# A hybrid encoder step on one core: the last stage joined to the experts' block, some of its rows gathered early, four of its tiles summed by TensorE

## The chip, the cores and the metric

The kernel is one program on one core of a Trainium2 chip. The metric is the device time of one execution in microseconds (us); lower is better. The kernel before was timed in 3 runs, and one more execution was recorded by the profiler.

## The reference

One inference step of a one-layer encoder for 1024 prompt rows and 64 sample rows, 1088 rows of 1024 values. Three branches (stick-breaking attention, gated linear attention, cross-attention into a memory) are gated, merged and projected, and give `h`. Then every row goes to two of 32 experts (the best of 4 groups, the best two of its 8 experts), and the result is normed once more:

```python
h = h + moe(rmsnorm(h))       # sum over the row's two experts e_k of
                              #   w_k * ((silu(x @ wg[e_k]) * (x @ wu[e_k])) @ wd[e_k])
y = rmsnorm(h) * norm_final   # outputs y_prompt (1024 rows), y_sample (64 rows)
```

The change concerns the last two lines alone: the sum of the two experts' rows and the final norm.

## The kernel before, in words

Rows are cut into nine tiles of 128 partitions (`NT = 9`; the last tile, number 8, has the 64 sample rows, `rows_of(t)`). The program is a chain of stages. A stage (`Stage`, line 51) has its own semaphores and one block of five instruction streams, one for each engine; at its end all engines meet at barriers and the semaphores are cleared (`Stage.clear`, line 63).

The last stage but one (lines 1754 to 2677) merges the branches, routes the rows and computes the experts. After routing, each expert has a slot of 128 rows in the DRAM tensor `expert_rows` (`ysd`); `sidx[k]` holds, for every row of the step, the line of `ysd` at which its k-th expert's result stands (`slots`, line 2629, run on VectorE within expert 14), and `wts` holds its two weights. Slots from 32 on are for experts with more than 128 rows; they are worked off by the loop in `further` (line 1778), whose bodies run only if there are such rows. In the profiled execution there were none.

For each expert n POOL gathers the slot's rows (`xe`, line 1892), SP loads the weights in halves (`raw`, 1 MB each, order `halves` on line 1715: gate, up of expert n, down of expert n-1; eight buffers, freed by the semaphore `used`, which TensorE raises when it has used a half), ScalarE rounds each half to `hig` (line 2238), VectorE subtracts to get `low` (line 2508), and TensorE multiplies in three passes (lines 2066 to 2068 and 2092 to 2094). ScalarE copies the expert's result out of PSUM into `ye` and stores it into `ysd` from its own DMA queue (line 2314). The last expert's result goes out in two halves (`last_out`, lines 2316 to 2326). At the end of the block ScalarE waits until all stores have landed (lines 2367 and 2368).

The last stage (lines 2687 to 2744) runs over the nine tiles:

- SP loads the final gain `gf` (line 2696), and stores each tile when it is scaled (line 2700).
- POOL gathers for each tile two sets of rows, `ya` and `yb`, from `ysd` by `sidx` (line 2708): 18 gathers of 128 rows of 4 KB (64 rows for tile 8).
- VectorE forms `ya * w0 + h` (line 2728) and then `yb * w1 + ya` (line 2731), both f32 over 1024 columns (`add`).
- ScalarE squares and sums the row, takes logarithm and exponential of the half for the inverse root (lines 2717 to 2721).
- VectorE multiplies the row with its root and `gf` into `yo` (line 2737, `scale`), one tile behind `add`.

## Time and profile before

| | us |
|---|---|
| median of 3 runs | 1832.4 |
| lowest, highest | 1829.63, 1832.93 |
| profiled execution, its own time | 1830.22 |
| span of the profiled execution, first to last instruction | 1828.5 |

| engine | busy, us | share of the span |
|---|---|---|
| TensorE (PE) | 1751.3 | 96% |
| VectorE (DVE) | 1055.0 | 58% |
| ScalarE (ACT) | 867.6 | 47% |
| GpSimd (POOL) | 111.7 | 6% |

The shares are means over stages with different limits; TensorE is idle in the last fortieth of the span or so. PEld is TensorE's weight load, PEq, ACTq, POOLq and SPq are the engines' sequencers, which issue DMAs. PEclk is the clock that TensorE was granted, as a share of full speed. The DMA share is the mean busy share of the core's 16 DMA engines; it can come out a little over 1. "Landing" is the time from the issue of a DMA until its semaphore says that all of it has arrived. Times within the trace count from the start of the span.

### The profile page before, as it was taken

How to read it: one execution, taken by the hardware profiler on the slowest of the kernel's cores; microseconds unless marked ns; L12 is line 12 of the kernel's file. 1: busy time of each engine (PE TensorE's matmuls, PEld its weight loads, DVE VectorE, ACT ScalarE, POOL GpSimd, SP SyncE). 2: the span in 40 equal slices, each digit the busy share in tenths (PEclk: the TensorE clock that was granted, in tenths of full speed). 3: DMA queues.
4: the chain of work that ended last, by engine and by line, in shares of the span. 5: the costliest groups of instructions: out<-in, count | busy, mean ns of one | idle time of the engine just before them, and what ended most of it. 6: DMA issues, size and time to landing. Idle time of an engine off the chain costs nothing. (4 is left out here: it accounts for less than half of the span.)

```text
span 1828.5 us, 25561 instructions
## 1 busy us (share of the span) xinstructions
PE 1751.3 (96%) x10338; PEld 1557.1 (85%) x10338; DVE 1055.0 (58%) x1285; ACT 867.6 (47%) x1122; POOL 111.7 (6%) x130
## 2 busy tenths in 40 slices
PE   8999999999999999999999999989999999999980
PEld 7888887989898899999999988878888888888870
DVE  5336664533354432142333155678988998898967
ACT  4225555332444331121122133258888888888753
POOL 0010000000000010000000000010001110000003
PEclk9999999999999999999999999989999999999995
DMA  5231111102022122222222152189999999999968
GB/s 190 82 107 41 30 31 42 30 24 74 24 73 81 47 73 80 65 87 70 75 80 65 35 186 82 53 316 400 416 412 410 414 416 419 417 415 408 415 228 304
DMA packets 139321, 329.85 MB, mean 180 GB/s; under 512 B 13674, under 2 KB 91334, under 8 KB 114501
## 3 DMA queue, kind: packets, MB, share of 16 engines
q1 hardware_dynamic: 123556, 272.69, 40.2%
q0 software_dynamic: 10896, 38.74, 5.6%
q10 hardware_dynamic: 4752, 16.78, 2.3%
q8 instruction: 84, 1.38, 0.3%
q14 instruction: 33, 0.27, 0.0%
HBM read 286.08 MB, written 39.87 MB: 178 GB/s over the span
## 5 line engine op out<-in xcount | busy, mean ns | idle before, releaser
L2508 DVE TENSOR_TENSOR low<-raw,hig 128x2048 fp32r<-128x2048 f32 x192 | 431.7, 2286 | 57.6 <-ACT hig L2238 57.4
L2238 ACT ACTIVATE hig<-raw 128x2048 fp32r<-128x2048 f32 x192 | 360.6, 1916 | 31.3 <-DMA raw<-in_w_e_gate_dram 14.9
L2066 PE MATMUL bank<-hig,xel 128*128 128x512 f32 x512 | 202.5, 396 | 0.5 <-DVE xel L2579 0.5
L2068 PE MATMUL bank<-hig,xeh 128*128 128x512 f32 x512 | 199.9, 390 | 0.0
L2067 PE MATMUL bank<-low,xeh 128*128 128x512 f32 x512 | 199.3, 389 | 0.0
L70 PE MATMUL bank<-xhi,glo 128*128 128x384 f32 (+1 forms) x552 | 180.6, 327 | 1.9 <-PEq L65 1.9
L72 PE MATMUL bank<-xhi,ghi 128*128 128x384 f32 (+1 forms) x552 | 180.8, 327 | 0.0
L71 PE MATMUL bank<-xlo,ghi 128*128 128x384 f32 (+1 forms) x552 | 180.5, 327 | 0.0
L70 PE MATMUL gproj<-xhi,glo 128*128 128x384 f32 (+1 forms) x384 | 130.1, 339 | 0.0
L72 PE MATMUL gproj<-xhi,ghi 128*128 128x384 f32 (+1 forms) x384 | 125.3, 326 | 0.0
L71 PE MATMUL gproj<-xlo,ghi 128*128 128x384 f32 (+1 forms) x384 | 125.2, 326 | 0.0
L2068 PEld LDWEIGHTS bank<-hig,xeh 128*128 128x128 f32 x512 | 96.1, 188 | 20.5
L2066 PEld LDWEIGHTS bank<-hig,xel 128*128 128x128 f32 x512 | 96.6, 189 | 19.6 <-DVE xel L2579 0.8
L2067 PEld LDWEIGHTS bank<-low,xeh 128*128 128x128 f32 x512 | 96.3, 188 | 19.0
L2401 DVE TENSOR_TENSOR tm<-sg,bank 128x384 f32<-128x384 f32 (+1 forms) x42 | 22.3, 531 | 152.5 <-PE bank L72 152.5
L70 PEld LDWEIGHTS bank<-xhi,glo 128*128 128x128 f32 x552 | 104.2, 189 | 2.0 <-issue 2.0
L71 PEld LDWEIGHTS bank<-xlo,ghi 128*128 128x128 f32 x552 | 104.2, 189 | 0.0
L72 PEld LDWEIGHTS bank<-xhi,ghi 128*128 128x128 f32 x552 | 104.0, 188 | 0.0
L2092 PE MATMUL bank<-hig,htl 128*128 128x512 f32 x256 | 102.4, 400 | 0.0
L2094 PE MATMUL bank<-hig,hth 128*128 128x512 f32 x256 | 100.0, 390 | 0.0
L2093 PE MATMUL bank<-low,hth 128*128 128x512 f32 x256 | 99.9, 390 | 0.0
L2172 ACT ACTIVATE sg<-bank 128x384 f32<-128x384 f32 (+1 forms) x63 | 29.7, 471 | 145.6 <-PE bank L72 136.6
(432 smaller groups left out, 3556.6 us busy)
## 6 DMA issues: line engine op xcount, KB each, us to landing
raw<-in_w_e_gate_dram SPq DMA_DIRECT2D x64, 1024.0 KB, 8.3
raw<-in_w_e_up_dram SPq DMA_DIRECT2D x64, 1024.0 KB, 8.5
raw<-in_w_e_down_dram SPq DMA_DIRECT2D x64, 1024.0 KB, 7.8
graw<-in_w_in_dram SPq DMA_DIRECT2D x39, 512.0 KB, 3.7
expert_rows<-ye ACTq DMA_DIRECT2D x31, 512.0 KB, 8.3
xt<-in_x_prompt_dram SPq DMA_DIRECT2D x16, 512.0 KB, 3.6
expert_rows<-nil POOLq DMA_DIRECT2D x16, 512.0 KB, 4.1
braw<-in_w_branch_dram SPq DMA_DIRECT2D x24, 256.0 KB, 3.0
```

The source lines that it names most:

```text
L70: nc.tensor.matmul(out, wl, xh, start=(opens and i == 0), stop=False)
L71: nc.tensor.matmul(out, wh, xl, start=False, stop=False)
L72: last = nc.tensor.matmul(out, wh, xh, start=False, stop=(closes and i == len(parts) - 1))
L2066: nc.tensor.matmul(bank[:, :], xel[n % 2][:, kk, :], wh[:, k, :], start=(kk == 0), stop=False)
L2067: nc.tensor.matmul(bank[:, :], xeh[n % 2][:, kk, :], wl[:, k, :], start=False, stop=False)
L2068: last = nc.tensor.matmul(bank[:, :], xeh[n % 2][:, kk, :], wh[:, k, :], start=False, stop=(kk == KC - 1))
L2092: nc.tensor.matmul(bank[:, :], htl[n % 2][:, kk, :], wh[:, k, cols], start=(kk == 0), stop=False)
L2093: nc.tensor.matmul(bank[:, :], hth[n % 2][:, kk, :], wl[:, k, cols], start=False, stop=False)
L2094: last = nc.tensor.matmul(bank[:, :], hth[n % 2][:, kk, :], wh[:, k, cols], start=False, stop=(kk == 3))
L2172: nc.scalar.activation(gate_of(i, g)[:, 0:m], src[:, 0:m], ACT.Sigmoid).then_inc(gated, 1)
L2238: nc.scalar.activation(hig[q % HI][:, :], raw[q % RAW][:, :], ACT.Copy).then_inc(high, 1)
L2508: nc.vector.tensor_tensor(low[q % RAW][:, :], raw[q % RAW][:, :], hig[q % HI][:, :].bitcast(F32), ALU.subtract).then_inc(lowed, 1)
```

## The change

The last stage's block is joined to the experts' block: no clearing and no barriers lie between them. Each engine's part stands behind its `further`, and the order is kept by semaphores. TensorE raises `closed` when its own work is done; SP then loads `gf`, ScalarE loads its table and VectorE begins. ScalarE raises `written` when every store into `ysd` has landed.

- **Gathers.** `LATE` is 3712, the first line of expert 29. For tiles 0 to 5 (`TWICE = 6`) POOL gathers twice. First, once the last two weight halves have landed and the stores of experts 0 to 28 too, it gathers by `sidx` with `bounds_check = LATE - 1`: lines beyond are left as they are. These rows go into buffers of the experts' block that have become free (`rows_at` gives each buffer and the value of `used` that frees it). After `written` it gathers again by `lidx`, in which the lines below `LATE` have 2^20 added and are so out of range. Tiles 6 to 8 are gathered once, after `written`. That makes 12 gathers before and 18 after `written`, where there were 18.
- **`slots`** computes `lidx`: two more small operations with a `drain` each, and two more copies, on VectorE.
- **Sums.** Tiles 1, 3, 5 and 7 (`ON_PE`) are summed by TensorE in PSUM: identity times `h`, plus a diagonal of the weights times `ya`, plus another times `yb`, each in two halves of 512 columns, all f32. VectorE builds the eight 128x128 diagonals `dg`. ScalarE and VectorE then read these tiles' sums from PSUM. VectorE adds the other five tiles as before, and scales two tiles behind instead of one.
- **PSUM** is declared as four tensors of 1024 columns in place of eight of 512; the addresses are the same.
- **Buffers** of `further`'s loop are moved to other places.

The diff, without the declarations that only move buffers:

```diff
-    psum = [top.enter_context(nc.psum_tensor(f"bank{i}", [P, 512], F32)) for i in range(8)]
-    PA, PB, TB, Z0, Z1, A0, A1, OB = psum
+    banks = [top.enter_context(nc.psum_tensor(f"banks{i}", [P, 1024], F32)) for i in range(4)]
+    PA, PB, TB, Z0, Z1, A0, A1, OB = [banks[i // 2][:, 512 * (i % 2):512 * (i % 2) + 512] for i in range(8)]
...
+    lidx = [at("lidx", [P, NT], I32, CON + 1024 + 64 * k) for k in range(2)]
...
+    LATE = (NE - 3) * P
+    TWICE = 6
+    spent = lambda kind, n, h: place[kind, n, h] + 1
+    rows_at = [(e0, 0), (e0 + 4096, 0), (e0 + 8192, spent("u", NE - 2, 1)), (e0 + 16384, spent("u", NE - 2, 1))]
+    for kind, h in (("g", 0), ("g", 1), ("u", 0), ("u", 1)):
+        q = place[kind, NE - 1, h]
+        rows_at += [(raw_at[q % RAW] + 4096 * i, q + 1) for i in range(2)]
+        if kind == "u":
+            rows_at += [(hig_at[q % HI] + 4096 * i, q + 1) for i in range(2)]
+    rows_at += [(e0 + 12288, spent("u", NE - 1, 1)), (e0 + 20480, spent("u", NE - 1, 1))]
+    assert len(rows_at) == 2 * NT
+    ya = [at("ya", [P, D], F32, rows_at[2 * t][0]) for t in range(NT)]
+    yb = [at("yb", [P, D], F32, rows_at[2 * t + 1][0]) for t in range(NT)]
+    ys_ = [nc.alloc_semaphore(name=f"rows_in{t}") for t in range(NT)]
+    yo = [at("yo", [P, D], F32, 4096 * i if i < FULL else OS) for i in range(NT)]
+    gf = at("gf", [P, D], F32, OS + 4096)
+    junk = at("junk", [P, D], F32, OS + 8192)
+    ON_PE = [1, 3, 5, 7]
+    dg = at("dg", [P, 2 * len(ON_PE), P], F32, OS + 12288)
+    landed = lambda t: 64 if t < TWICE else 32
     fours = lambda t: t[:, :].rearrange("p (k n) -> p k n", k=4)
...
+            sp.wait_ge(closed, 1)
+            sp.dma_start(gf[:, :], io["norm_final"].partition_broadcast(P)).then_inc(norm_in, 16)
+            for t in range(NT):
+                r = rows_of(t)
+                sp.wait_ge(finished, t + 1)
+                sp.dma_start(yp[t * P:t * P + r, :] if t < FULL else ysm[:, :], yo[t][0:r, :]).then_inc(returned, 16)
+            sp.wait_ge(returned, 16 * NT)
...
+            pool.wait_ge(found, 1)
+            pool.wait_ge(s0, 16 * (LATE // P + 1) // 2)
+            pool.wait_ge(s1, 16 * (LATE // P // 2))
+            for q in range(len(halves) - 2, len(halves)):
+                pool.wait_ge(loaded[q % RAW], 16 * (q // RAW + 1))
+            for t in range(TWICE):
+                r = rows_of(t)
+                for k, dst in enumerate((ya, yb)):
+                    pool.wait_ge(used, rows_at[2 * t + k][1])
+                    pool.indirect_dma_start(dst[t][0:r, :], None, ysd[0:LATE, :],
+                                            bass.IndirectOffsetOnAxis(ap=sidx[k][0:r, t:t + 1], axis=0),
+                                            bounds_check=LATE - 1, oob_is_err=False).then_inc(ys_[t], 16)
...
+            pool.wait_ge(written, 1)
+            for t in range(NT):
+                r = rows_of(t)
+                if t < TWICE:
+                    pool.wait_ge(ys_[t], 32)
+                for k, dst in enumerate((ya, yb)):
+                    rows = (lidx if t < TWICE else sidx)[k]
+                    pool.indirect_dma_start(dst[t][0:r, :], None, ysd,
+                                            bass.IndirectOffsetOnAxis(ap=rows[0:r, t:t + 1], axis=0),
+                                            bounds_check=SLOTS - 1, oob_is_err=False).then_inc(ys_[t], 16)
...
+            pe.sem_inc(closed, 1)
+            pe.wait_ge(written, 1)
+            pe.wait_ge(diagonal, 1)
+            for j, t in enumerate(ON_PE):
+                for half in range(2):
+                    out, c = banks[j][:, 512 * half:512 * half + 512], slice(512 * half, 512 * half + 512)
+                    if half == 0:
+                        pe.wait_ge(ys_[t], landed(t))
+                    nc.tensor.matmul(wide(out), ident[:, :], hrow(t, P)[:, 4 * half:4 * half + 4, :], start=True, stop=False)
+                    nc.tensor.matmul(out, dg[:, 2 * j, :], ya[t][:, c], start=False, stop=False)
+                    last = nc.tensor.matmul(out, dg[:, 2 * j + 1, :], yb[t][:, c], start=False, stop=True)
+                last.then_inc(added, 1)
...
+            act.sem_inc(written, 1)
+            act.wait_ge(closed, 1)
+            nc.scalar.preload_act_table_set("natural_log_exp_and_others")
+            for t in range(NT):
+                R = slice(0, rows_of(t))
+                if t in ON_PE:
+                    act.wait_ge(added, ON_PE.index(t) + 1)
+                    total = banks[ON_PE.index(t)]
+                else:
+                    act.wait_ge(summed, t + 1 - sum(u < t for u in ON_PE))
+                    total = ya[t]
+                nc.scalar.activation(junk[R, :], total[R, :], ACT.Square, scale=D ** -0.5, accum_out=stat[R, t:t + 1])
+                act.drain()
+                nc.scalar.activation(stat[R, 16 + t:17 + t], stat[R, t:t + 1], ACT.Ln, bias=eps[R, :])
+                act.drain()
+                nc.scalar.activation(stat[R, 32 + t:33 + t], stat[R, 16 + t:17 + t], ACT.Exp, scale=-0.5).then_inc(inverted, 1)
...
+                nc.vector.tensor_scalar(isov[:, :, :], eid[:, :, :], float(LATE), float(1 << 20), ALU.is_lt, ALU.mult)
+                ve.drain()
+                nc.vector.tensor_tensor(isov[:, :, :], isov[:, :, :], eid[:, :, :], ALU.add)
+                ve.drain()
                 for k in range(2):
-                    last = nc.vector.tensor_copy(sidx[k][:, :], eid[:, :, k])
+                    nc.vector.tensor_copy(sidx[k][:, :], eid[:, :, k])
+                    last = nc.vector.tensor_copy(lidx[k][:, :], isov[:, :, k])
                 last.then_inc(found, 1)
...
-    ya = [at("ya", [P, D], F32, OS + 8192 * i) for i in range(NT)]
-    yb = [at("yb", [P, D], F32, OS + 8192 * i + 4096) for i in range(NT)]
-    yo = [at("yo", [P, D], F32, 4096 * i) for i in range(NT)]
...
-    with Stage(nc) as ctx:
...
-            for t in range(NT):
-                r = rows_of(t)
-                for k, dst in enumerate((ya, yb)):
-                    pool.indirect_dma_start(dst[t][0:r, :], None, ysd,
-                                            bass.IndirectOffsetOnAxis(ap=sidx[k][0:r, t:t + 1], axis=0)).then_inc(ys_[t], 16)
...
+            ve.wait_ge(closed, 1)
             def add(t):
                 r = rows_of(t)
-                ve.wait_ge(ys_[t], 32)
+                ve.wait_ge(ys_[t], landed(t))
...
             def scale(t):
                 r = rows_of(t)
-                ve.wait_ge(rooted, t + 1)
-                nc.vector.scalar_tensor_tensor(out=yo[t][0:r, :], in0=ya[t][0:r, :], scalar=stat[0:r, 32 + t:33 + t],
+                ve.wait_ge(inverted, t + 1)
+                total = banks[ON_PE.index(t)] if t in ON_PE else ya[t]
+                nc.vector.scalar_tensor_tensor(out=yo[t][0:r, :], in0=total[0:r, :], scalar=stat[0:r, 32 + t:33 + t],
                                                in1=gf[0:r, :], op0=ALU.mult, op1=ALU.mult).then_inc(finished, 1)
-            ve.wait_ge(g_in, 16)
-            for t in range(NT + 1):
-                if t < NT:
+            for j, t in enumerate(ON_PE):
+                for k in range(2):
+                    last = nc.vector.tensor_scalar(dg[:, 2 * j + k, :], ident[:, :], wts[:, t, k:k + 1], None, ALU.mult)
+            last.then_inc(diagonal, 1)
+            ve.wait_ge(norm_in, 16)
+            for t in range(NT + 2):
+                if t < NT and t not in ON_PE:
                     add(t)
-                if t >= 1:
-                    scale(t - 1)
+                if t >= 2:
+                    scale(t - 2)
```

## Rows read from the trace of the kernel before

**Rows 1.** Busy by windows: us; PE, PEld, DVE, ACT, POOL busy; PEclk, DMA share, GB/s

```profile
1469.00:1481.00 12.00, 12.00 (x56) 9.99 (x55) 11.70 (x16) 9.24 (x9) 0.00 (x0) 1.00 1.01 417
...
1764.50:1773.80 9.30, 9.30 (x44) 7.53 (x43) 5.23 (x4) 3.20 (x4) 0.00 (x0) 1.00 0.00 1
...
1780.00:1781.00 1.00, 0.00 (x0) 0.00 (x0) 0.00 (x0) 0.00 (x0) 0.00 (x0) 0.54 0.24 88
...
1790.00:1796.00 6.00, 0.00 (x0) 0.00 (x0) 5.82 (x5) 2.48 (x5) 4.73 (x5) 0.50 1.00 367
...
1800.00:1812.00 12.00, 0.00 (x0) 0.00 (x0) 11.78 (x11) 5.50 (x15) 4.67 (x5) 0.50 1.03 420
```

**Rows 2.** The chain that ended last, in order of time: start us, us, what

```profile
1783.01 0.94 POOL ya L2708
...
1784.26 5.45 DMA yb<-expert_rows,sidx
...
1821.40 1.06 ACT junk L2717
...
1823.22 1.28 DVE yo L2737
```

**Rows 3.** Second addition, line 2731: duration ns min/median/max, starts, forms

```profile
L2731 DVE SCALAR_TENSOR_TENSOR ya<-yb,wts,ya x9: 1275/1283/1285, 1791.2 to 1820.1; 128x1024 f32<-128x1024 f32 x8, 64x1024 f32<-64x1024 f32 x1
```

**Rows 4.** Gathers of the last stage, line 2708: duration ns min/median/max, starts, landing

```profile
L2708 POOL DMA_INDIRECT ya<-expert_rows,sidx x9: 919/948/1397, 1783.0 to 1803.8; - x9
...
L2708 POOL DMA_INDIRECT yb<-expert_rows,sidx x9: 910/949/1066, 1784.3 to 1805.0; - x9
...
  issue: 5.2, 17
...
DMA to landing us min/median/max: 4.5/5.8/12.4
```

**Rows 5.** Timeline, end of experts: start us, us, engine line op [idle before <-releaser]

```profile
1763.57 0.39 PE L2066 MATMUL bank<-hig,xel 128*128 128x512 f32 x1
...
1763.96 4.48 DVE L2508 TENSOR_TENSOR low<-raw,hig 128x2048 fp32r<-128x2048 f32 x2
...
1764.09 1.92 ACT L2238 ACTIVATE hig<-raw 128x2048 fp32r<-128x2048 f32 x1 [0.61 <-DMA raw<-in_w_e_down_dram]
...
1773.81 0.34 ACTq L2314 DMA_DIRECT2D expert_rows<-ye  x1
...
1777.65 0.39 PE L2094 MATMUL bank<-hig,hth 128*128 128x512 f32 x1
...
1778.70 0.34 ACTq L2326 DMA_DIRECT2D expert_rows<-ye  x1
```

**Rows 6.** Gathers of the experts' loop, line 1892: duration ns min/median/max

```profile
L1892 POOL DMA_INDIRECT xe<-ffn_rows,toks x32: 942/1368/3187, 1202.1 to 1714.4; - x32
```

**Rows 7.** Landing: the experts' stores (line 2314), the last (line 2326), gf (line 2696)

```profile
DMA to landing us min/median/max: 2.6/8.3/10.6
...
DMA to landing us min/median/max: 2.0/2.0/2.0
...
DMA to landing us min/median/max: 3.8/3.8/3.8
```

**Rows 8.** f32 matmuls of 512 columns: timeline of four records; durations of line 1129

```profile
561.48 1.88 PE L1129 MATMUL gout<-pT,mn 128*128 128x512 f32 x4
...
L1129 PE MATMUL gout<-pT,mn x16: 592/592/595, 561.5 to 644.6; 128*128 128x512 f32 x16
```

**Rows 9.** Busy time by windows at the kernel's start; columns as in rows 1

```profile
12.00:13.00 1.00, 1.00 (x4) 0.77 (x3) 1.00 (x2) 1.00 (x1) 0.00 (x0) 0.50 1.02 393
...
15.00:16.00 1.00, 1.00 (x5) 0.82 (x4) 0.73 (x2) 0.87 (x2) 0.00 (x0) 0.80 1.06 389
```

**Rows 10.** ScalarE reading 1024 columns of PSUM, line 1293 (form 128x1024)

```profile
L1293 ACT ACTIVATE osq<-gout,stat x6: 360/1114/1116, 394.8 to 522.7; 128x1024 f32<-128x1024 f32 x4, 128x128 f32<-128x128 f32 x2
```

**Rows 11.** A small operation of slots, line 2641

```profile
L2641 DVE TENSOR_TENSOR eid<-eid,isov x1: 178/178/178, 1475.5 to 1475.5; 128x18 f32<-128x18 f32 x1
```

More of the change, by code:

```diff
@@ L1769, in build @@
                 ctx, "o", "t in g u d turned copied hidden silued mult hturned hcopied down read out passed")
+        norm_in, diagonal, summed, added, inverted, finished, returned, closed, written = sems(
+            ctx, "z", "norm_in diagonal summed added inverted finished returned closed written")
+        ctx.held += ys_
+        yp = io["out0"].rearrange("b t d -> (b t) d")
+        ysm = io["out1"].rearrange("b t d -> (b t) d")
         g_in, b_in, x_in, kept = [g_in0, g_in1], [b_in0, b_in1], [x0, x1], [kept0, kept1]
@@ L2677, in _ @@
             further(ve, body)
-    ya = [at("ya", [P, D], F32, OS + 8192 * i) for i in range(NT)]
-    yb = [at("yb", [P, D], F32, OS + 8192 * i + 4096) for i in range(NT)]
-    yo = [at("yo", [P, D], F32, 4096 * i) for i in range(NT)]
-    gf = at("gf", [P, D], F32, 36864)
-    junk = at("junk", [P, D], F32, 40960)
-    with Stage(nc) as ctx:
-        g_in, summed, rooted, finished, stored, *ys_ = sems(
-            ctx, "z", "g_in summed rooted finished stored " + " ".join(f"y{t}" for t in range(NT)))
-        block = ctx.enter_context(nc.Block())
-        yp = io["out0"].rearrange("b t d -> (b t) d")
-        ysm = io["out1"].rearrange("b t d -> (b t) d")
-        @block.sync
-        def _(sp):
-            sp.dma_start(gf[:, :], io["norm_final"].partition_broadcast(P)).then_inc(g_in, 16)
-            for t in range(NT):
-                r = rows_of(t)
-                sp.wait_ge(finished, t + 1)
-                sp.dma_start(yp[t * P:t * P + r, :] if t < FULL else ysm[:, :], yo[t][0:r, :]).then_inc(stored, 16)
-            sp.wait_ge(stored, 16 * NT)
-        @block.gpsimd
-        def _(pool):
-            for t in range(NT):
-                r = rows_of(t)
-                for k, dst in enumerate((ya, yb)):
-                    pool.indirect_dma_start(dst[t][0:r, :], None, ysd,
-                                            bass.IndirectOffsetOnAxis(ap=sidx[k][0:r, t:t + 1], axis=0)).then_inc(ys_[t], 16)
-        @block.scalar
-        def _(act):
-            nc.scalar.preload_act_table_set("natural_log_exp_and_others")
-            for t in range(NT):
-                R = slice(0, rows_of(t))
-                act.wait_ge(summed, t + 1)
-                nc.scalar.activation(junk[R, :], ya[t][R, :], ACT.Square, scale=D ** -0.5, accum_out=stat[R, t:t + 1])
-                act.drain()
-                nc.scalar.activation(stat[R, 16 + t:17 + t], stat[R, t:t + 1], ACT.Ln, bias=eps[R, :])
-                act.drain()
-                nc.scalar.activation(stat[R, 32 + t:33 + t], stat[R, 16 + t:17 + t], ACT.Exp, scale=-0.5).then_inc(rooted, 1)
-        @block.vector
-        def _(ve):
```

12 lines of the change are left out of this document (6 added, 6 removed).

## The prediction, made before the changed kernel ran

> **What bounds the kernel now.** I read the windows over the end first, then the chain, then the timeline around the hand-over, and last the groups of single lines. The experts' block is bound by TensorE until 1778.0 and the change leaves that part alone, but for some small operations in `slots`. From the last weights on the DMA engines have nothing to do: share 0.00 from 1764.5 to 1773.8, while TensorE works through the last expert [rows 1]. Then come the hand-over and the last stage. The reader should see in the chain that POOL's first gather starts at 1783.01, that its pair lands at about 1789.7 and that VectorE's last scaling starts at 1823.22 [rows 2]: with its 1.28 us it ends at 1824.5, and the span ends 4.0 us later, at 1828.5. So the last stage is 41.5 us from first gather to last VectorE instruction. In it VectorE is busy for 11.78 of 12 us [rows 1]: each tile costs it two additions and a scaling of 1.28 us each, nine tiles at 3.75 us [rows 2, 3]. POOL needs 0.95 us plus an idle 0.30 us for a gather, 2.5 us for a tile [rows 4], so it runs ahead.
>
> **The sum, part by part.** g is the start of POOL's first gather after the hand-over; times are those of the trace.
>
> Early gathers. Twelve, tiles 0 to 5. The last raw half has landed when ScalarE starts on it at 1764.09 [rows 5]; the stores of experts 0 to 28 landed well before, as that of 29 was issued two experts' time ago, and the buffers of tiles 4 and 5 come free when TensorE ends the first half of expert 31's `up`, at about 1763.6 [rows 5]. At 1.25 us each [rows 4] POOL issues them until 1779.3; at 1.37 + 0.30 us, the median of the gathers in the experts' loop [rows 6], until 1784.1. VectorE, whose work goes with the long ones, has two splits left until 1768.4 [rows 5], so I take 1780. They move up to 6.3 MB in DMA time that stood empty.
>
> The hand-over. Before: last store issued 1778.70, landed 2.0 us later [rows 5, 7], then the clearing of semaphores, the barriers, POOL's start at 1783.01. After: the store, two semaphores, POOL. With free DMA engines g would be 1781.2. But the stores of experts 30 and 31 (issued 1773.8 and, its last half, 1778.7 [rows 5]) now share the engines with gathers that fill them: 1.00 of the DMA share with gathers alone [rows 1]. Bounds for one store: 2.0 us alone, and 8.3 us, the median of those beside the weight loads [rows 7]. At 367 GB/s [rows 1] 5.7 MB of rows and 1.0 MB of stores take 18.3 us from 1764.5, until 1782.8. I take 3.3 us, g = 1782.5: 0.5 us won of 1.8. The Trainium skill, DMA: Bandwidth & Descriptors, section Queues, rings and completion order, has a DMA engine go round its queues a packet at a time. By that a store waits for about one packet of the gathers on each engine, near the short bound; the 8.3 us of this trace speak against it, so both stay.
>
> Late gathers. Eighteen in place of eighteen, twelve of them with nine rows in ten out of range. POOL's time for such a row isn't in the trace. The 64-row gathers took 0.91 to 0.92 us, as good as the 128-row ones [rows 4], so fewer rows hardly save; I take 1.25 us, bounds 0.9 and 1.67 [rows 6]. Landing from issue: 4.5 us at least for full ones [rows 4], 2.0 us for a small store; I take 3.5. Tile t's second gather starts at g + 1.25(2t+1): tile 0 is there at 1787.3, tile 1 at 1789.8, tile 3 at 1794.8, tile 5 at 1799.8. Tiles 6 to 8 are full and meet the output stores; before, landings reached 12.4 us [rows 4]. I take 7: tile 7 at 1808.3, tile 8 at 1810.8.
>
> TensorE's sums. Six f32 matmuls of 512 columns a tile. Such a matmul shows as two records; four records took 1.88 us and one takes 0.592, so (1.88 - 0.59) / 3 = 0.43 us from one to the next [rows 8]. A tile is 12 x 0.43 = 5.2 us at 2.4 GHz. But the granted clock fell to 0.5 at about 1780.1, 2 us after the last matmul [rows 1, 5], and at the start of the kernel it stood at 0.50 from 12 to 15 while matmuls ran without a pause, and was back in the slice from 15 to 16, by its 0.80 at about 15.4 [rows 9]. So I charge tile 1 with 4 us at half speed: 2 us more, 7.2 us, ready at 1797.0. Then tile 3 at 1802.2, tile 5 at 1807.4, tile 7 (waits for its rows, 1808.3) at 1813.5. TensorE, idle here before, is now as much a limit as POOL.
>
> ScalarE. From the square to VectorE's scaling 1.82 us [rows 2]; a 1024-wide read of PSUM took 1.11 us where the one of SBUF takes 1.06 [rows 2, 10], nothing to count. It takes the tiles in order, so tile 8 waits behind 7: 1815.3, 1817.1. `gf` and its table load now come before the rows (issue after `closed`, about 1779.5, landing 3.8 us later [rows 7]; VectorE waits for `gf` before its first addition, and has till 1787.3). If it lands 3 us late among gathers, nothing is lost.
>
> VectorE. Ten additions in place of eighteen and nine scalings: 19 x 1.25 = 24 us instead of 34. Its cover is gone: it now waits for TensorE's tiles through ScalarE. `add(8)` ends at 1813.5, `scale(6)` at 1814.8, `scale(7)` at 1816.6, `scale(8)` 1817.1 + 1.28 = 1818.4. The eight diagonals (128x128) fall into its empty time before 1787. The four small operations and two drains in `slots` cost some 0.9 us at 0.18 us each [rows 11], in a stretch where VectorE is 11.70 of 12 us busy and TensorE still never stops [rows 1]: hidden, at worst 0.9 us.
>
> The end. 4.0 us as now, plus 0.3 for stores that follow closer. 1818.4 + 4.3 = 1822.7 against 1828.5: **5.8 us less**. The profiled execution took 1830.2 us, so 1824.4; it is 2.2 us below the median of the runs shown, 1832.4. Against the median: **1826.6 us**, -0.32%. A measurement tells about 0.2% from nothing, 3.7 us. With the cheap ends of the bounds (store 2.0, landing 2.0 and 4.5) the end is some 10 us earlier: 1822.
>
> **Rivals.**
> A, slower: TensorE's clock stays at 1.2 GHz through its four tiles. It works in bursts with waits for rows between, after a long idle, and a drop needed only the 2 us of 1778 to 1780 [rows 1, 5]. Then a tile costs 10.3 us, tile 7 is ready at 1789.8 + 41.2 = 1831.0, `scale(8)` ends at 1836, the span at 1840: 12 us more, 1844. It decides from about 7.4 us a tile on: then the last scaling stands where it stood. For it: clock 0.50 over the whole last stage. Against it: dense matmuls brought the clock back in 4 us [rows 9], and by my sum TensorE hardly pauses. The Trainium skill, TensorE: Matmul & The Clock Gate, section Part 1: The HAM clock gate, says that sustained work brings the full clock back; the trace agrees at 15.4. 0.10.
> B, range-checked gathers are dear: 1.67 us each on POOL. Early ones until 1784.1, g = 1784.4, late ones 5 us more; tile 7's rows at 1815.2, its sum 1820.4, last scaling 1825.3, end 1829.6: 1833.5, no change, and slower beyond that price. For it: the median 1.37 us in the experts' loop, up to 3.19 [rows 6]. Against: 0.95 us in the last stage although VectorE was busy throughout [rows 1, 4]. The Trainium skill, GPSIMD Engine Reference, section Key points, says that GpSimd's ports to SBUF are shared with VectorE's two-input instructions. VectorE's additions have two inputs and the gathers beside them were short, so the trace bears it out only in part. 0.16, a third of it slower.
> C, the early gathers hold up the last stores: 8.3 us as in the weight stream [rows 7]. Last store down at 1787.0, g = 1787.2, end 4.7 us later than forecast: 1831.3, no change. For it: a DMA share of 1.00. Against: the backlog should be gone by 1783. 0.14.
> D, the twelve late gathers still move all their rows: then DMA is full, but 8.9 MB of gathers and 4.5 MB of stores at 420 GB/s [rows 1] are 32 us from g, 1814.5, still inside POOL's and TensorE's pace. 1 to 2 us less gain. 0.04.
>
> **How the numbers follow.** The forecast (with D) has 0.60, most of it between 1822 and 1828.7; B 0.16, C 0.14, A 0.10. Faster: 0.60 x 0.92 and a few hundredths of B and C make 0.60. Same: 0.24. Slower: A 0.10, a third of B 0.05 and 0.01 of C make 0.16. The range runs from 1821.5 to 1835.0: it holds the forecast with both ends of its bounds, C, and B at its price, and leaves out A, B at more than its price, and a gain over 11 us.
>
> **What the profile of after would show.** Twelve gathers from 1764 to 1780; DMA share near 1 there; the last store landing by 1782; the first late gather at 1782.5; late gathers 1.25 us apart; f32 records 0.43 us apart after some 4 us at 0.85; a chain that changes between TensorE, ScalarE and VectorE, with no 3.75 us period; last scaling ending near 1818. The prediction falls if records stay 0.85 us apart (A), if POOL's period is over 1.6 us (B), or if the first late gather starts after 1786 (C).

## The result and the profile after

The changed kernel is slower: over 20 timed executions of each kernel on the same chips the median went from 1830.97 to 1838.48 us, and the ratio is 1.0035 with a 95% interval of 1.0026 to 1.0043. The forecast was 0.32% faster, with a range up to 1835.0; both the sign and the range missed. The ratios here are taken over executions in the ordinary, fast state: a few single ones that took far longer (3479.3 us of the kernel before, 1918.84 of e2, 2517.09 and 4504.99 of e8) are left out of them, though not out of the medians. The profiled execution took 1836.51 us, its span 1834.9 (before: 1830.22 and 1828.5).

The first view is the busy time by windows of the changed kernel (columns as in rows 1).

```profile
1766.00:1768.00 2.00, 2.00 (x10) 1.65 (x9) 2.00 (x2) 0.53 (x1) 1.79 (x1) 1.00 0.00 0
1768.00:1770.00 2.00, 2.00 (x11) 1.43 (x10) 1.69 (x2) 0.00 (x0) 1.87 (x1) 1.00 0.71 178
1770.00:1780.00 10.00, 8.68 (x40) 6.90 (x39) 0.69 (x1) 2.88 (x5) 7.59 (x8) 1.00 0.88 290
1780.00:1790.00 10.00, 0.00 (x0) 0.00 (x0) 1.66 (x8) 1.28 (x1) 3.27 (x4) 0.55 1.01 397
1790.00:1800.00 10.00, 3.91 (x5) 1.83 (x6) 4.02 (x4) 1.65 (x4) 7.56 (x9) 0.50 0.18 43
1800.00:1810.00 10.00, 10.00 (x22) 4.22 (x21) 6.26 (x6) 3.80 (x9) 7.87 (x8) 0.92 0.54 149
1810.00:1820.00 10.00, 6.01 (x13) 2.47 (x12) 7.26 (x6) 5.75 (x16) 2.60 (x3) 0.93 0.97 369
```

Read the DMA share down the column. The empty stretch before the hand-over is filled as intended, though only from 1768 on. But a new hole has opened where there was none: 0.18 from 1790 to 1800 and 0.54 after it, where the kernel before had 1.00 and 1.03 [rows 1]. VectorE is no longer the busy engine there (4.02 and 6.26 of 10 us; it was 11.78 of 12 before [rows 1]). POOL is: 7.56 and 7.87 us, which with 0.30 us between gathers is all of its time.

The timeline around the hand-over (start us, us, engine, line):

```profile
1765.58 2.22 POOL L1937 DMA_INDIRECT ya<-expert_rows,sidx  x1 [49.20 <-DMA expert_rows<-ye]
1768.10 1.87 POOL L1937 DMA_INDIRECT yb<-expert_rows,sidx  x1 [0.30 <-issue]
...
1779.35 0.34 ACTq L2393 DMA_DIRECT2D expert_rows<-ye  x1
1779.41 1.00 POOL L1937 DMA_INDIRECT yb<-expert_rows,sidx  x1 [0.30 <-issue]
...
1782.03 1.06 POOL L1937 DMA_INDIRECT yb<-expert_rows,sidx  x1 [0.30 <-issue]
1788.47 1.28 ACT L2438 ACT_TABLE_LOAD   x1 [9.16 <-DMA expert_rows<-ye]
1789.21 1.00 POOL L1957 DMA_INDIRECT ya<-expert_rows,lidx  x1 [6.12 <-ACTq L2436]
```

Twelve early gathers (line 1937), nine of them issued before the last store at 1779.35. ScalarE then waits 9.2 us for that store and only then gives `written`; the first late gather (line 1957), called g as in the prediction, starts at 1789.21, 9.9 us after the store's issue, against 4.3 before (1783.01 less 1778.70, [rows 2, 5]).

The chain that ended last answers to rows 2:

```profile
1779.35 9.04 DMA expert_rows<-ye
...
1807.55 1.78 POOL ya L1957
1809.64 8.77 DMA yb<-expert_rows,sidx
1818.45 1.99 PE banks L2209 x2
...
1825.60 1.02 ACT junk L2447
...
1829.06 1.27 DVE yo L2780
```

Before, this chain was VectorE's additions and scalings. Now it is the store's landing, then POOL's gathers one behind the other, then the landing of tile 7's rows, then TensorE's sum of that tile. The group of the late gathers (answers to rows 4; its landings are those of full ones) and the landing of `gf` (the last line, from its own group; [rows 7]):

```profile
L1957 POOL DMA_INDIRECT ya<-expert_rows,lidx x6: 1001/1001/1018, 1789.2 to 1802.3; - x6
L1957 POOL DMA_INDIRECT yb<-expert_rows,lidx x6: 997/1000/1053, 1790.5 to 1803.6; - x6
L1957 POOL DMA_INDIRECT ya<-expert_rows,sidx x3: 963/999/1783, 1804.9 to 1811.0; - x3
L1957 POOL DMA_INDIRECT yb<-expert_rows,sidx x3: 948/1001/1053, 1806.2 to 1812.3; - x3
...
DMA to landing us min/median/max: 8.2/8.5/8.9
...
DMA to landing us min/median/max: 7.9/7.9/7.9
```

A gather that leaves out most of its rows costs POOL the same 1.00 us as a full one; what it saves is DMA time only. Its rows are there soon: TensorE began tile 1 at 1796.09, 3.0 us after that tile's second gather was issued at 1793.13. That is how the hole from 1790 to 1800 comes about: twelve nearly empty gathers (`lidx`) keep POOL for 12 x 1.31 = 15.7 us and give the DMA engines almost nothing, and the six full ones stand behind them. The DMA queues from 1764 to the end show that no row is moved twice (queue, kind: packets, MB, share); first the changed kernel, then the one before from 1780 on:

```profile
q0 software_dynamic: 4192, 8.92, 38.4%
```

```profile
q0 software_dynamic: 2464, 8.91, 48.6%
```

TensorE's sums, timeline of line 2209 to 2211; each row of two records is one f32 matmul of 512 columns:

```profile
1796.09 2.04 PE L2209 MATMUL banks<-mixT,ident 128*128 128x512 f32 x2 [17.40 <-DMA yb<-expert_rows,lidx]
1797.92 1.91 PE L2210 MATMUL banks<-ya,dg 128*128 128x512 f32 x2
...
1801.34 1.11 PE L2209 MATMUL banks<-mixT,ident 128*128 128x512 f32 x2
1802.28 1.02 PE L2210 MATMUL banks<-ya,dg 128*128 128x512 f32 x2
...
1818.45 1.99 PE L2209 MATMUL banks<-mixT,ident 128*128 128x512 f32 x2 [3.99 <-DMA yb<-expert_rows,sidx]
...
1821.95 1.04 PE L2211 MATMUL banks<-yb,dg 128*128 128x512 f32 x2
```

At half clock a matmul takes 1.71 us, at the full one 0.86. The clock rose after 5.2 us of work (granted clock 0.62 in the window 1800 to 1802, 1.00 from 1802 on). It fell again at the end of TensorE's wait of 3.99 us for tile 7's rows: 1.00 until 1818.5, 0.57 from 1818.5 to 1819, 0.50 until 1821.5.

### The profile page after: what moved, and what is told of

Its sections match the earlier page's. It is cut to its first block, busy times and chain, and to the rows that moved or that the text cites. A ratio compares the mean times of both kernels' runs of the same rounds, so it can differ in the third digit from the quotient of the medians.

```text
span 1834.9 us, 25681 instructions
## 1 busy us (share of the span) xinstructions
PE 1778.3 (97%) x10386; PEld 1569.0 (86%) x10386; DVE 1047.5 (57%) x1289; ACT 867.5 (47%) x1122; POOL 134.5 (7%) x142
## 4 chain that ended last, share of the span: by engine, by line
PE 59%; DMA 2%; issue 1%; POOL 1%; DVE 0%; ACT 0%; DVEq 0%; ACTq 0%; POOLq 0%
PE banks L70 7%; PE banks L72 7%; PE banks L71 7%; PE banks L2121 6%; PE banks L2123 6%; PE banks L2122 6%; PE banks L2149 3%; PE banks L2147 3%; PE banks L2148 3%; PE banks L2004 2%; PE banks L2006 2%; PE banks L2005 2%; PE banks L2107 2%; PE banks L2131 1%; PE banks L2034 1%
## 5 line engine op out<-in xcount | busy, mean ns | idle before, releaser
L2121 PE MATMUL banks<-hig,xel 128*128 128x512 f32 x512 | 202.5, 396 | 0.5 <-DVE xel L2662 0.5
L2123 PE MATMUL banks<-hig,xeh 128*128 128x512 f32 x512 | 199.9, 390 | 0.0
L2122 PE MATMUL banks<-low,xeh 128*128 128x512 f32 x512 | 199.3, 389 | 0.0
L70 PE MATMUL banks<-xhi,glo 128*128 128x384 f32 (+1 forms) x552 | 179.9, 326 | 1.9 <-PEq L65 1.9
L72 PE MATMUL banks<-xhi,ghi 128*128 128x384 f32 (+1 forms) x552 | 180.0, 326 | 0.0
L71 PE MATMUL banks<-xlo,ghi 128*128 128x384 f32 (+1 forms) x552 | 179.9, 326 | 0.0
L70 PEld LDWEIGHTS banks<-xhi,glo 128*128 128x128 f32 x552 | 103.6, 188 | 2.0 <-issue 2.0
L72 PEld LDWEIGHTS banks<-xhi,ghi 128*128 128x128 f32 x552 | 103.6, 188 | 0.0
L71 PEld LDWEIGHTS banks<-xlo,ghi 128*128 128x128 f32 x552 | 103.6, 188 | 0.0
L2147 PE MATMUL banks<-hig,htl 128*128 128x512 f32 x256 | 102.4, 400 | 0.0
```

What stands on the lines that cost most here:

```text
L70: nc.tensor.matmul(out, wl, xh, start=(opens and i == 0), stop=False)
L71: nc.tensor.matmul(out, wh, xl, start=False, stop=False)
L72: last = nc.tensor.matmul(out, wh, xh, start=False, stop=(closes and i == len(parts) - 1))
L2121: nc.tensor.matmul(bank[:, :], xel[n % 2][:, kk, :], wh[:, k, :], start=(kk == 0), stop=False)
L2122: nc.tensor.matmul(bank[:, :], xeh[n % 2][:, kk, :], wl[:, k, :], start=False, stop=False)
L2123: last = nc.tensor.matmul(bank[:, :], xeh[n % 2][:, kk, :], wh[:, k, :], start=False, stop=(kk == KC - 1))
```

## The experiments

The experts' block does the same work in all of them, early gathers aside, but ends at another time in each trace (the last store's issue, called s here, lies between 1777.1 and 1782.9), so profiled executions are compared from s to the end of the span. Each such figure comes from one execution. The verdict is the ratio to the kernel before on the same chip; it is not the quotient of the medians shown. Two theories stood against each other. S: the early gathers hold up the last store, and with it `written` and all the late gathers. O: the order of the late gathers, empty ones first and full ones last, wastes the DMA engines and brings tile 7's rows late.

| kernel | gathers issued before s | store landed after | g - s | end - g | end - s | median us | ratio to before (95%) |
|---|---|---|---|---|---|---|---|
| before | 0 | 2.0 | 4.3 | 45.5 | 49.80 | 1830.97 | 1 |
| after | 9 | 9.0 | 9.9 | 45.7 | 55.55 | 1838.48 | 1.0035 (1.0026 to 1.0043) |
| e1_no_early | 0 | 2.0 | 2.9 | 47.8 | 50.69 | 1831.62 | 0.9998 (0.9989 to 1.0007) |
| e2_early3 | 6 | 4.0 | 4.8 | 44.6 | 49.47 | 1831.88 | 0.9998 (0.9989 to 1.0007) |
| e3_join_only | 0 | 2.0 | 2.9 | 46.2 | 49.04 | 1830.21 | 0.9997 (0.9988 to 1.0005) |
| e4_no_pe | 10 | 8.8 | 9.7 | 45.5 | 55.15 | 1836.37 | 1.0027 (1.0017 to 1.0036) |
| e5_warm | 10 | 9.9 | 10.7 | 48.0 | 58.69 | 1837.86 | 1.0029 (1.0017 to 1.0041) |
| e6_mixed | 6 | 4.0 | 4.8 | 43.9 | 48.72 | 1829.02 | 0.9983 (0.9974 to 0.9992) |
| e7_split | 6 | 4.1 | 8.7 | 46.6 | 55.23 | 1836.69 | 1.0024 (1.0015 to 1.0034) |
| e8_mixed2 | 4 | 2.0 | 2.8 | 45.3 | 48.14 | 1830.75 | 0.9990 (0.9980 to 0.9999) |
| e9_half_stores | 0 | 2.0 | 2.9 | 43.0 | 45.89 | 1828.37 | 0.9980 (0.9970 to 0.9991) |
| e10_split4 | 6 | 3.7 | 4.5 | 43.2 | 47.69 | 1828.26 | 0.9983 (0.9974 to 0.9992) |
| e11_early4 | 8 | 7.9 | 8.8 | 46.7 | 55.51 | 1836.22 | 1.0025 (1.0015 to 1.0036) |
| e12_full_first | 9 | 8.8 | 9.6 | 39.4 | 49.06 | 1830.56 | 0.9992 (0.9983 to 1.0001) |

(In `before`, g is the first gather of the last stage.) Where the tiles go in their natural order and all outputs are stored, the end comes 44.6 to 48.0 us after g, whatever was gathered early and whoever sums: 45.5 before, 45.7 after. So the 5.75 us that the changed kernel loses from s on are almost all its late g (9.9 for 4.3), and nothing that the early gathers and TensorE were to bring behind g arrived.

**The three parts one by one.** The change joins the stages, gathers early, and sums on TensorE. e1 takes the early gathers away, e2 halves them, e3 leaves only the joining, e4 only takes TensorE's sums away (e3 and e4 also drop the semaphore `diagonal`).

```diff
-    TWICE = 6
-    ON_PE = [1, 3, 5, 7]
+    TWICE = 0            # e1; 3 in e2; 0 in e3; 6 in e4
+    ON_PE = [1, 3, 5, 7] # e1, e2; [] in e3 and e4
```

> The changed kernel with TWICE = 0: no gather before the last stores, all nine tiles gathered once after them; all else as changed. Theory S (the early gathers and the gain's load keep the DMA engines full until 1789, and the last store's landing goes from 2.0 to 9.0 us): the last store lands in about 2 us again, the first late gather starts near 1782.2 instead of 1789.2, tile 7's sum by TensorE is ready near 1817, span about 1826, that is some 8 us under the changed kernel and 2 us under the one before. Rival K (the sums on TensorE, with its clock at half speed twice, are what costs): the span stays above 1832 though the gathers start earlier.

> The changed kernel with TWICE = 3: six early gathers instead of twelve. Theory S: they are issued from 1765.6 to about 1775 and drained by about 1777, before the last two stores are issued, so these land in 2 to 3 us and the first late gather starts near 1782.5; tiles 0 to 2 are then there at once, tile 7 as in the run without early gathers; span 1825 to 1826. Rival K: above 1832. If the delay of the store does not depend on the backlog (any gather on that queue delays it), the first late gather starts near 1789 as with twelve.

> TWICE = 0 and no tile on TensorE: only the blocks are joined, VectorE adds all nine tiles. Theory S: first gather near 1782.2 against 1783.0 before, then the same 3.75 us a tile: span about 1827.5, 1 us under the kernel before. It gives the price of the barrier between the stages. Rival: joining costs by itself (queues or semaphores): span above 1830.

> The changed kernel with TWICE = 6 kept and no tile on TensorE. Theory S: first late gather near 1789.2 as changed, tile 0 at 1793.3, then nine tiles at 3.75 us and 1.8 us of ScalarE with the last scaling: last scaling ends near 1830, span about 1834, within 1 us of the changed kernel. Rival K: taking TensorE out brings the span to 1829 or less.

The chains of e1 and of e2, from the last store to the rows of tile 7:

```profile
1779.31 2.02 DMA expert_rows<-ye
...
1802.75 10.75 DMA yb<-expert_rows,sidx
```

```profile
1779.13 4.01 DMA expert_rows<-ye
...
1803.65 10.19 DMA yb<-expert_rows,sidx
```

Both ended later than S had them (1830.0 and 1828.6, where about 1826 was expected), and below rival K's 1832. All of the loss belongs to the early gathers: without them the changed kernel runs as the one before, with all twelve it loses 0.35%, and with TensorE's sums or without them (after and e4) the intervals overlap. Joining the stages brings the first late gather 1.4 us nearer to the store (2.9 for 4.3), but in e3 the span ends 4.55 us after the last scaling where it was 4.00, and e3 as a whole cannot be told from before. And e1 shows why TensorE brings nothing: VectorE has 5.61 us of work in 10 (1790 to 1800), yet the rows of tile 7 land 10.75 us after their gather, because the DMA engines are full. Its windows:

```profile
1790.00:1800.00 10.00, 7.44 (x12) 3.33 (x13) 5.61 (x5) 1.65 (x4) 7.90 (x7) 0.63 1.00 387
1800.00:1810.00 10.00, 9.89 (x24) 4.14 (x23) 6.86 (x6) 6.30 (x16) 5.43 (x5) 1.00 0.99 371
```

**Is DMA the bound of the last stage?** e9 is e1 with only 512 of the 1024 columns of the two row outputs stored; it leaves half of those outputs out.

```diff
-                sp.dma_start(yp[...] if t < FULL else ysm[:, :], yo[t][0:r, :]).then_inc(returned, 16)
+                sp.dma_start((yp[...] if t < FULL else ysm[:, :])[:, 0:512], yo[t][0:r, 0:512]).then_inc(returned, 16)
```

> As e1_no_early, but only the first 512 of the 1024 columns of each output row are stored (2.2 MB instead of 4.5 MB; the other half of the two outputs is left out); all gathers and sums stay. If the DMA engines are the limit of the last stage (share 0.99 to 1.00 from 1790 to 1810 in e1_no_early, tile 7's rows landing 10.7 us after their issue): tile 7's rows land some 5 us earlier, TensorE does not wait for them, and from the last store's issue to the end of the span it is 46 us instead of 50.7. If TensorE's or POOL's pace is the limit: 50 us or more.

From s to the end it took 45.89 us, 4.8 less than e1, and the median fell by 3.3 us. No engine but the DMA had less to do. The 2.23 MB less at the 387 GB/s of e1's window would be 5.8 us. So with VectorE relieved the DMA engines bound this stage. In the kernel before they ran at 1.00 and 1.03 in the same stretch [rows 1], behind a VectorE that never paused; that they stood close behind it there is argued from these shares, since the kernel before was not run with half of its stores.

**More work for TensorE's clock.** e5 is the changed kernel with nine more matmuls (`warm`), whose results are overwritten later: five behind `written`, four ahead of tile 7.

```diff
             pe.wait_ge(diagonal, 1)
...
+            warm(5)
             for j, t in enumerate(ON_PE):
+                if j == 3:
+                    warm(4)
```

> The changed kernel with nine f32 matmuls of 512 columns added on TensorE into the bank of tile 7, which is overwritten later: five after `written`, four before tile 7. In the changed kernel the granted clock was 0.50 when tile 1's rows came, and fell again in the 4.0 us wait for tile 7's rows, whose sum then took 7.1 us instead of 5.2. Theory (the second fall is worth 1.9 us, the first nothing, because tile 7 waits for its rows anyway): from the issue of the last store to the end of the span 53.7 us instead of 55.6, tile 1 in about 5.2 us instead of 7.5. Rival (the clock costs 4 us in all): 51.5 us. If the added matmuls do not hold the clock: 55.6 or more.

The first sum did run at the full clock, but 53.7 us from s to the end were expected and 58.69 came. Timeline of TensorE in e5:

```profile
1795.38 1.13 PE L2215 MATMUL banks<-mixT,ident 128*128 128x512 f32 x2 [0.29 <-DMA yb<-expert_rows,lidx]
...
1819.52 2.08 PE L2215 MATMUL banks<-mixT,ident 128*128 128x512 f32 x2 [4.43 <-DMA yb<-expert_rows,sidx]
```

Tile 7's rows landed 10.5 us after their issue at 1808.94, and the clock fell in the wait for them (0.64 in 1817 to 1818) in spite of the four matmuls ahead, which had ended at 1815.1. The two medians (1837.86 and 1838.48) differ by less than their spread. The clock in the first sum is off the path: what decides is when tile 7's rows are there, and whether the clock has fallen by then. That the sums before it, ended earlier, put their output stores in the way of these rows fits, but is argued only.

**What does the store wait for?** e7 keeps twelve early gathers but holds the six of tiles 3 to 5 back until the last store is issued; e11 has eight in the old place.

```diff
                     pool.wait_ge(used, rows_at[2 * t + k][1])
+                    if t == 3:
+                        pool.wait_ge(emptied, NE)    # e7, e10
```

> The changed kernel, where POOL's last six early gathers (tiles 3 to 5) wait until the last expert's result has left PSUM, so that they are issued just behind the last store instead of ahead of it. If the DMA engines serve what was queued first (a store waits for the bytes queued before it): the last store lands in about 4.0 us, as with six early gathers, though six more follow. If a store shares the engines with gathers whenever they were queued: 7 to 9 us. In the first case the first late gather is held up by POOL's own six gathers, starting 8 to 8.5 us after the store's issue instead of 9.9: span about 1 to 2 us under the changed kernel.

> The changed kernel with TWICE = 4: eight early gathers, all ahead of the last store. The landing of the last store has been 2.0 us with none and with four, 4.0 with six, 9.0 with twelve. If it waits for what is queued before it, two more gathers of 0.95 MB in all at 0.38 MB per us add 2.5 us: 6.0 to 6.7 us, first late gather 7 us after the store's issue. If there is a threshold instead of a backlog: 4.0 or 9.0.

The landing of the last store in e7 and in e11:

```profile
DMA to landing us min/median/max: 4.1/4.1/4.1
```

```profile
DMA to landing us min/median/max: 7.9/7.9/7.9
```

Six gathers behind the store do not touch it in e7 (4.1, as e2 with none behind: 4.0). Those issued before it do, and steeply: 2.0 with none or four, 3.7 to 4.1 with six, 7.9 with eight, 8.8 to 9.9 with nine or ten. That is S's mechanism. For e11, 6.0 to 6.7 us were expected from a backlog, and 4.0 or 9.0 from a threshold; 7.9 is neither. The bytes that the queues moved show why it is steep:

| kernel | gathers ahead of s | rows moved until s, MB | moved from s to the landing: rows, all, MB | landing, us |
|---|---|---|---|---|
| e8 | 4 | 1.89 | 0, 0.35 | 2.0 |
| e2 | 6 | 2.49 | 0.38, 1.36 | 4.0 |
| e7 | 6 | 2.56 | 0.45, 1.14 | 4.1 |
| e11 | 8 | 2.54 | 1.30, 2.44 | 7.9 |
| after | 9 | 2.54 | 2.49, 3.60 | 9.0 |
| e5 | 10 | 3.09 | 2.57, 3.70 | 9.9 |

An early gather moves 0.48 MB (3.84 MB for the eight of e11). Until s the engines got through about 2.5 MB of rows, that is five gathers, in e11 and the changed kernel alike; what is issued beyond that ahead of the store stands whole in front of it. In the changed kernel 1.8 MB of the nine gathers were left at s, and 2.49 MB of rows moved before the store landed, so there rows issued behind it went along with it. In e7, where 0.3 MB were left, hardly any did.

A short landing alone does not help. The landing of e7 was 4.9 us shorter than that of the changed kernel, but g came only 1.2 us sooner and the end 0.3 us. The timeline of POOL in e7 shows why:

```profile
1779.09 1.00 POOL L1939 DMA_INDIRECT ya<-expert_rows,sidx  x1 [4.99 <-ACT ye L2393]
...
1785.62 1.00 POOL L1939 DMA_INDIRECT yb<-expert_rows,sidx  x1 [0.30 <-issue]
1786.93 1.00 POOL L1959 DMA_INDIRECT ya<-expert_rows,lidx  x1 [0.30 <-issue]
```

The six moved gathers occupy POOL until 1786.6, and the late ones, empty first, follow at the same 1.31 us: tile 7's second gather was issued 29.3 us after s, in the changed kernel 30.3. What counts is when POOL can begin its late gathers, and what stands in its queue ahead of the full ones. Where g itself moves, the end follows: e2 has g 4.0 us nearer to s than e11, and its end 6.0 us nearer.

**The order.** e12 is the changed kernel with the late gathers in another order, full tiles between empty ones (TensorE takes tiles 0, 1, 2 and 4 in it). SP, POOL, ScalarE and VectorE all follow the list.

```diff
-    ON_PE = [1, 3, 5, 7]
+    QUEUE = [6, 0, 7, 1, 8, 2, 3, 4, 5]
+    ON_PE = [0, 1, 2, 4]
...
-            for t in range(NT):
+            for t in QUEUE:
```

> The changed kernel with its twelve early gathers, so with the late last store (about 9 us, first late gather about 9.9 us after its issue), but the order of work after it is 6, 0, 7, 1, 8, 2, 3, 4, 5: the three tiles that move all their rows come first, when the DMA engines are empty and no output is being stored; TensorE's tiles stay at places 2, 4, 6 and 8 of the nine. Theory O (the changed kernel loses the second half of its time because its full gathers come last, behind output stores, and land 8.8 us after their issue): no wait for rows at the end, from the last store's issue to the end of the span about 49 to 50 us instead of 55.6, which puts it level with the kernel before (49.8). Theory S alone (the late store is the whole loss, the order does not matter): 55 us or more.

The chain of e12 (the store, then the first and the last of TensorE's matmuls) and its windows:

```profile
1781.94 8.81 DMA expert_rows<-ye
...
1798.64 2.05 PE banks L2210 x2
...
1815.83 1.46 PE banks L2212 x2
```

```profile
1790.00:1800.00 10.00, 1.35 (x2) 0.84 (x3) 1.73 (x2) 1.28 (x1) 6.58 (x7) 0.50 0.78 268
1800.00:1810.00 10.00, 10.00 (x20) 4.20 (x19) 6.39 (x6) 4.80 (x12) 7.59 (x8) 0.83 0.64 192
1810.00:1820.00 10.00, 10.00 (x25) 4.41 (x24) 9.01 (x8) 5.71 (x14) 4.63 (x4) 1.00 0.57 195
```

The store lands as late as in the changed kernel (8.8 us), all twelve early gathers are there, and still 6.5 us are gone: 49.06 us from s to the end instead of 55.55, a ratio of 0.9992 instead of 1.0035. From g to the end it is 39.4 us instead of 45.7, and the share in the first window after the hand-over went from 0.18 to 0.78. So both theories hold, each for its part. S is why the changed kernel is slower than the one before; O is why twelve early gathers and TensorE's sums gained nothing behind g; and mending either alone brings the kernel level with before (e2, e12). The next limit in e12 is TensorE, whose four sums follow each other without a pause from 1798.64 to 1817.3. That only the order of the full gathers matters, and not the choice of TensorE's tiles that had to go with it, was not taken apart.

**Versions that use this.** e6: three tiles early, full ones between the empty ones (order 0, 3, 1, 4, 2, 5, 6, 7, 8; TensorE 3, 4, 5, 7). e8: two early (order 0, 2, 1, 3, 4, 5, 6, 7, 8; TensorE 0, 1, 4, 6; two warming matmuls). e10: four early, the fourth held back as in e7 (order 0, 4, 1, 5, 2, 6, 3, 7, 8; TensorE 0 to 3).

> As e2_early3 (six early gathers), but the order of work is 0, 3, 1, 4, 2, 5, 6, 7, 8 in place of 0 to 8, with the tiles of TensorE at the same places in that order. Theory O (in e2_early3 POOL spent 7.8 us of DMA engines nearly empty, share 0.19 from 1784 to 1790, on gathers that move little, and then the full ones met the output stores at a share of 1.0, landing 9.0 us): the full gathers start earlier, landings fall to about 6 us, from the last store's issue to the end of the span 45 to 46.5 us instead of 49.5. Rival (POOL's 1.30 us a gather or TensorE's 5.2 us a tile is the limit, whatever the order): 49 us or more.

> A version meant to beat both: TWICE = 2 (four early gathers), order of work 0, 2, 1, 3, 4, 5, 6, 7, 8, TensorE sums tiles 0, 1, 4 and 6 (places 0, 2, 4 and 6, so that the last full tile is VectorE's), two added f32 matmuls to raise its clock. Theories S and O together: last store lands in 2 to 2.5 us, first late gather 3 us after its issue, landings 5 to 7 us, from the last store's issue to the end of the span 42 to 45 us, against 49.8 before and 55.6 changed. Rival: if the DMA engines are full anyway from 1790 on (8.9 MB of gathers less 1.9 MB, and 4.5 MB of stores), 47 us or more.

> A version meant to beat both: four early tiles, of which the fourth (two gathers) is issued just behind the last store; order of work 0, 4, 1, 5, 2, 6, 3, 7, 8; TensorE sums tiles 0 to 3, whose rows are mostly there. If a store waits for the bytes queued before it: it lands in 4.0 us as with three early tiles, the first late gather starts 4.8 us after its issue, and one more tile (0.95 MB, 2.4 us of DMA) is out of the late stretch: 46 to 47.5 us from the last store's issue to the end of the span, against 48.7 in e6_mixed, 49.8 before and 55.6 changed; ratio to the kernel before about 0.997. Rival: the two gathers behind the store hold it up too: first late gather 6 us or more after it, 48.5 us or more.

All three fell short of what was expected from s to the end: 48.72 us in e6 (45 to 46.5), 48.14 in e8 (42 to 45) and 47.69 in e10 (46 to 47.5, at a ratio of 0.997). With six early gathers the order is worth little: e6 differs from e2 in it alone (TensorE's tiles stand at the same places) and ends 0.75 us nearer to s; by the ratios (0.9983 and 0.9998) it may be up to 3 us, but their intervals overlap.

In e10's chain the last store and the landing of tile 7's rows, then its windows:

```profile
1777.11 3.69 DMA expert_rows<-ye
...
1801.68 8.62 DMA yb<-expert_rows,sidx
```

```profile
1780.00:1790.00 10.00, 3.21 (x4) 1.50 (x5) 0.33 (x2) 1.28 (x1) 6.79 (x8) 0.50 0.83 264
1790.00:1800.00 10.00, 10.00 (x22) 4.32 (x21) 5.83 (x5) 3.15 (x8) 7.87 (x8) 0.89 0.72 204
1800.00:1810.00 10.00, 10.00 (x24) 4.20 (x23) 7.94 (x7) 6.30 (x16) 4.39 (x5) 1.00 0.96 332
```

e10 and e6 beat both kernels by a little: 0.9983 (0.9974 to 0.9992), some 3 us below before and 10 us below the changed kernel. That is just under the 0.2% that was named as telling, though the interval leaves 1 out. e8 is at 0.9990 (0.9980 to 0.9999). Beside e11, which has the same four tiles early, e10 gains 8 us by the order and the held-back pair together. Even here POOL is busy without a pause and the DMA share is 0.72 from 1790 to 1800, so part of the DMA time that the early gathers won still goes unused while POOL works through its queue.

## Why the prediction was wrong, step by step

It had the last VectorE instruction end at 1818.4 and the span at 1822.7; they were 1830.3 and 1834.9. (Its base, a median of 1832.4 from three runs, was 1.4 us above the median over 20.) The 12.2 us between divide over its terms:

| term | predicted | measured | us |
|---|---|---|---|
| g, the first late gather | 1782.5 | 1789.21 | +6.7 |
| tile 7's rows, from g | 25.8 | 29.2 | +3.4 |
| TensorE's sum of tile 7 | 5.2 | 7.1 | +1.9 |
| end of that sum to the end of the last scaling | 4.9 | 4.8 | -0.1 |
| tail | 4.3 | 4.6 | +0.3 |

- **The hand-over (+6.7), the step that failed most.** I took 3.3 us for the store between bounds of 2.0 and 8.3; it took 9.0, beyond the upper end. Of the 6.7 us that is 5.7; 0.65 is a last store issued later in this trace, and 0.3 the way from landing to g (0.8 for 0.5). The bound was a median; the same row had landings of up to 10.6 [rows 7]. That is rival C's mechanism, to which I gave 0.14, at a g 2.0 us later than its 1787.2 (which, with the sum's own 0.5 us, should have been 1787.5). The reason that I set against it, a backlog gone by 1783, was wrong in its start: I let the rows move from 1764.5, but POOL's first gather started at 1765.58 and with the second took 2.22 and 1.87 us, beside VectorE's splits, and nothing moved before 1768; the share was 0.88, not 1.00, from 1770 to 1780. By s the engines had moved 2.54 MB of rows and 1.8 MB of those issued were left. As an estimate, the same 18.3 us counted from 1768 end at 1786.3, and `gf` (0.5 MB, left out of the sum) adds 1.4: 1787.7, near the 1788.39 at which the store landed. The Trainium skill, DMA: Bandwidth & Descriptors, section Queues, rings and completion order, lets the engines go round their queues by packets, which as I read it would put the store near 2 us; no run with six or more gathers ahead of it bears that out (3.7 to 9.9). The same section has the increment of a semaphore land only after the earlier writes of that DMA engine, whatever their queue. That the gathers ahead of the store count (e2, e11) and six behind it don't (e7) agrees with it; in the changed kernel rows issued behind the store went along with it too, so it is not the whole account.
- **From g to the end (40.2 us forecast, 45.7 measured).** I had the path right: tile 7's sum waits for its rows, and these for POOL's queue of eighteen gathers, which the early ones relieve of bytes but not of one instruction. What I did not ask is what the DMA engines do while twelve nearly empty gathers stand ahead of the six full ones. Their share was 0.18 for 10 us, and the full ones then met the output stores. With the full ones put between the empty ones (e12) it took 39.4 us. The other rows of the table are how these 5.5 us show in the sum.
- **Tile 7's rows (+3.4).** Their gather was issued 20.4 us after g instead of 18.75: fifteen steps of 1.31 us, not 1.25, and one gather of 1.78. They then took 8.8 us to land, not 7, beside the output stores, at a share of 0.97 from 1810 on. In e1, e2 and e11 the same landing took 10.2 to 10.75 us; with half of the stores (e9) it took 8.4 instead of e1's 10.75.
- **The clock (+1.9).** Tile 1 went as forecast, 7.9 us for 7.2, but was not on the path. The sum at the end was, and there I had charged nothing for the clock, since "TensorE hardly pauses": it had waited 3.99 us for the rows when the clock fell. Rival A, a clock that stays low, is out: tiles 3 and 5 took 5.15 us each.
- **Right:** the price of a sum at full clock (5.15 us for 5.2), the half clock on tile 1 (5.2 us of it, for 4), the diagonals hidden (done by 1782.6), small landings for tiles 0 to 5 (3.0 us for tile 1, where I took 3.5), `gf` 7.9 us on its way and not waited for. Rival B's price was small: 1.00 + 0.30 us a range-checked gather where the plain one of before took 0.95 + 0.30. Rival D is out: 8.92 MB through the gathers' queue, as before.
- **What was overlooked in the profile of before.** Rows 1 show the last stage with VectorE at 11.78 of 12 us and DMA at 1.03. I named the first as the bound, rightly, and did not say that the second left no room behind it. e1, where TensorE takes four tiles, ends no sooner than e3, where VectorE keeps its work (50.69 and 49.04 us from s), and halving the stores gains (e9). A relief of VectorE could be worth little without relief of the DMA engines in the same stretch, and the way chosen to relieve them starved them just there.

Left open: how the engines share out rows issued behind a store, which went along with it in the changed kernel and hardly in e7; and how much of e10's gain is the order and how much the held-back pair.

## What to carry to other kernels

Work that is moved ahead of a hand-over gains little if it takes only bytes and no instruction off the queue that issues it: a gather that skips its rows cost its engine as much as a full one (1.00 us). When some of a queue's transfers are empty and some full, put the full ones first or between, so that the DMA engines are fed while the empty ones are issued (6.3 us from g to the end with twelve early gathers, little with six). Count what the DMA engines can move before a store on which others wait is issued, and issue no more than that ahead of it: about 2.5 MB here. And before an engine is relieved, read the other shares of the same window: VectorE's and the DMA engines' stood within a few per cent of each other here, and in e1 the second took the gain.

## What the runs showed that was not expected

- A 256 KB store issued behind six indirect gathers (3 MB) landed after 3.7 to 4.1 us, behind eight after 7.9, behind nine or ten after 8.8 to 9.9; six gathers issued right behind it changed nothing where the backlog was short (4.1). Of the rows issued ahead of it, about 2.5 MB had moved by then with eight and with nine gathers alike.
- An indirect gather with range check took POOL 1.00 us and 0.30 to the next, whether it moved 128 rows or about a tenth of them.
- The first two gathers beside VectorE's splits took 2.22 and 1.87 us, and the first moved no byte for 2.4 us (DMA share 0.00 from 1766 to 1768).
- TensorE's granted clock fell at the end of a wait of 3.99 us and came back after 3.5 us of matmuls at half speed (1818.45 to 1821.95); after the long idle of the hand-over it took 5.2 us (1796.09 to 1801.34).
